# Column sums in place of row sums for two norms, and keys scaled ahead of queries, in a one-core stack of mixers

## The reference, cut to what matters

```python
# gla: 4 heads, keys of 128, values of 256 channels, chunks of 64 tokens
q_dec = q * dk**-0.5 * exp(bcum);  k_inv = k * exp(-bcum);  k_dec = k * exp(b_last - bcum)
o = tril(q_dec @ k_inv.T) @ v + q_dec @ state;  state = state * exp(b_last) + k_dec.T @ v
o = rms_norm(o, o_gain)                      # over the 256 channels of a head, per token
y = (o * silu(z)) @ w_out
# gdn: 4 heads of queries and keys of 128 channels, 8 of values
q = l2_norm(q) * d**-0.5;  k = l2_norm(k)    # over the 128 channels of a head, per token
```

## Time and profile before

| | us |
|---|---|
| median of 3 runs (2366.01 to 2367.77) | 2366.65 |
| the profiled execution's own time | 2366.76 |
| its span, from the first instruction to the last | 2365.0 |
| TensorE busy, of the span | 2293.6 (97%) |
| VectorE, ScalarE, GpSimd busy | 1264.3, 1005.0, 773.2 |

### The profile page before, as it was taken

The page is one execution under the profiler, slowest core; times in us unless marked ns, Lnnn a source line. Parts: engine busy times, 40 slices in busy tenths (PEclk is TensorE's granted clock), DMA queues, the critical chain, the costliest instruction groups (busy, mean ns, idle before and its releaser), DMA issues. The chain is left out here.

```text
span 2365.0 us, 37170 instructions
## 1 busy us (share of the span) xinstructions
PE 2293.6 (97%) x14784; PEld 1947.7 (82%) x14784; DVE 1264.3 (53%) x2094; ACT 1005.0 (42%) x1674; POOL 773.2 (33%) x571
## 2 busy tenths in 40 slices
PE   9999999999999999999999989999999999999998
PEld 7877777878868878877787657999988888999986
DVE  6434246345635545533224774777754344777754
ACT  4335435143444544345424553544524323544522
POOL 3423344133420025333333413111264454111264
PEclk9999999999999999999999999999999999999999
DMA  5333222132210014432222112233233323233232
GB/s 152 72 71 72 82 89 89 37 74 83 89 54 3 3 38 96 92 72 50 87 89 72 64 45 72 90 108 106 89 107 108 104 93 107 90 107 106 89 107 89
DMA packets 137036, 191.93 MB, mean 81 GB/s; under 512 B 31024, under 2 KB 84656, under 8 KB 136896
## 3 DMA queue, kind: packets, MB, share of 16 engines
q1 hardware_dynamic: 128928, 183.64, 26.2%
q10 hardware_dynamic: 7968, 6.32, 0.9%
HBM read 187.84 MB, written 2.10 MB: 80 GB/s over the span
## 5 line engine op out<-in xcount | busy, mean ns | idle before, releaser
L818 POOL TENSOR_TENSOR weights_low<-weights_raw,weights_high 128x512 fp32r<-128x512 f32 x520 | 703.7, 1384 | 1212.7 <-ACT weights_high L1975 1212.6
L1975 ACT ACTIVATE weights_high<-weights_raw 128x1024 fp32r<-128x1024 f32 x260 | 260.9, 1050 | 385.3 <-PE bank L897 379.5
L895 PE MATMUL bank<-xt_high,weights_high 128*128 128x256 f32 (+1 forms) x1152 | 390.1, 339 | 3.9 <-ACT third_sum L2297 1.6
L897 PE MATMUL bank<-xt_high,weights_low 128*128 128x256 f32 (+1 forms) x1152 | 381.9, 332 | 0.0
L896 PE MATMUL bank<-xt_low,weights_high 128*128 128x256 f32 (+1 forms) x1152 | 381.2, 331 | 0.0
L895 PEld LDWEIGHTS bank<-xt_high,weights_high 128*128 128x128 f32 x1152 | 219.3, 190 | 32.9 <-issue 5.6
L897 PEld LDWEIGHTS bank<-xt_high,weights_low 128*128 128x128 f32 x1152 | 219.1, 190 | 21.2
L896 PEld LDWEIGHTS bank<-xt_low,weights_high 128*128 128x128 f32 x1152 | 219.5, 190 | 16.5
L895 PE MATMUL bank<-weights_high,xt_high 128*128 128x512 f32 x432 | 173.9, 403 | 4.9 <-DVE xt_low L2851 2.8
L897 PE MATMUL bank<-weights_high,xt_low 128*128 128x512 f32 x432 | 168.9, 391 | 0.0
L896 PE MATMUL bank<-weights_low,xt_high 128*128 128x512 f32 x432 | 168.7, 391 | 0.0
(11 more groups left out here) (481 smaller groups left out, 4807.0 us busy)
## 6 DMA issues: line engine op xcount, KB each, us to landing
weights_raw<-in_fox_w_in_dram SPq DMA_DIRECT2D x64, 512.0 KB, 5.7
weights_raw<-in_ffn_w_gate_dram SPq DMA_DIRECT2D x44, 512.0 KB, 4.0
weights_raw<-in_ffn_w_up_dram SPq DMA_DIRECT2D x44, 512.0 KB, 4.9
weights_raw<-in_ffn_w_down_dram SPq DMA_DIRECT2D x40, 512.0 KB, 4.3
weights_raw<-in_gla_w_in_dram SPq DMA_DIRECT2D x24, 512.0 KB, 4.5
weights_raw<-in_gdn_w_in_dram SPq DMA_DIRECT2D x24, 512.0 KB, 4.5
weights_raw<-in_attn_w_qkv_dram SPq DMA_DIRECT2D x24, 512.0 KB, 4.5
weights_raw<-in_conv_w_in_dram SPq DMA_DIRECT2D x24, 512.0 KB, 4.2
```

The costliest lines, as they stand in the source:

```text
L818: pool.tensor_tensor(w_lo[:, odd, k], raw[:, odd, k], w_hi[:, odd, k].bitcast(F32), ALU.subtract)\
L895: pe.matmul(out_ap, lh, rh, start=first, stop=False, skip_group_check=skip)
L897: return pe.matmul(out_ap, ll, rh, start=False, stop=last, skip_group_check=skip)
L1975: act.activation(w_hi[:, odd, 2 * m:2 * m + 2], raw[:, odd, 2 * m:2 * m + 2], ACT.Copy)\
```

## The change

- **Sums.** Each squared tile becomes the stationary operand, 128 tokens at a time, and a single column of ones moves (`column_sums`). There are 8 tiles of 4 blocks in each of the two stages, so 32 float32 matmuls with one moving column each. The sums then stand with tokens on the partitions: 128x16 in gla, where both tiles of a head add up in PSUM and DVE's four additions (L3410) go, and 128x32 in gdn.
- **Roots.** ACT does one square root on that tile in place of logarithm and exponential, with its table loaded earlier by `load_root_table`. DVE does a reciprocal, the three Newton operations and the split on 128x16 or 128x32 in place of 4x512 or 8x512 (`norm_columns`).
- **Turned back.** Four transposes on TensorE (`turn_factors`) and a copy of 64x512 from PSUM by DVE (`factor_rows`) bring the factors to rows for the spread, which now has 64 partitions in its contraction.
- **Order in gla.** DVE makes the keys of all heads first and the queries after. TensorE waits for the keys before the transposes and for the queries before `inside(0)`. ACT takes gate 4, loads the root table and squares the first 384 tokens of six tiles before the last output block is there. Gate pieces: (5,1), sums, (6,0), turn, (7,0), spread, (6,1), (7,1). DVE multiplies gates 0 to 2 ahead of the norm, 3 and 4 during it, and 5 after it.
- **Order in gdn.** Sums, values 0 and 1, (4,0), turn, values 2 and 3, spread of four, (4,1), the other values. DVE takes values 0 and 1 inside the norm and 2 and 3 after the first four products. ACT does the root between the two halves of the odd slot's high part.

```diff
+            def column_sums(st, squares, heads, dst):
+                n = max(heads) + 1
+                for k, (tile, h) in enumerate(zip(squares, heads)):
+                    pe.wait_ge(squares_done, st["squares"] + k + 1)
+                    for tt in range(TT):
+                        ins = pe.matmul(dst[:, n * tt + h:n * tt + h + 1], tile[:, tt * P:tt * P + P], ones[:, 0:1],
+                                        start=k == tt == 0, stop=k == len(heads) - 1 and tt == TT - 1,
+                                        skip_group_check=True)
                     ins.then_inc(squares_used, 1)
+            def turn_factors(st, dst):
+                pe.wait_ge(rows_r, st["norms"] + 1)
+                for tt in range(TT):
+                    ins = pe.transpose(dst[0:CHUNK, tt * P:tt * P + P], factor_columns[st["kind"]][:, tt].bitcast(F32), ident[:])
+                ins.then_inc(factors_turned, 1)
...
+                    pe.wait_ge(gla["keys"], 2 * GLA_HEADS)
                     inside(0)
...
                     gate_piece(5, 1)
-                    for h in range(GLA_HEADS):
-                        pe.wait_ge(squares_used, st["squares"] + 2 * h + 2)
-                        ins = pe.matmul(bank[2][0:GLA_HEADS], pick[:, 15 - h:15 - h + GLA_HEADS], buf_c[:, 2 * h],
-                                        start=h == 0, stop=h == GLA_HEADS - 1)
-                    ins.then_inc(gla["norm_sums"], 1)
+                    column_sums(st, [buf_c[:, n] for n in range(8)], [n // 2 for n in range(8)], bank[2])
                     gate_piece(6, 0)
+                    turn_factors(st, bank[2])
                     gate_piece(7, 0)
-                    gate_piece(6, 1)
-                    pe.wait_ge(gla["state"], 8)
-                    pe.wait_ge(rows_r, st["norms"] + 1)
+                    pe.wait_ge(gla["state"], 9)
                     for h in range(GLA_HEADS):
                         spread(st, h, gla["spread"], bank[4 + h])
+                    gate_piece(6, 1)
                     gate_piece(7, 1)
...
-                    norm_sums(st, list(range(8)), 8, bank[1])
+                    column_sums(st, [scratch(st)["squares"][:, n % 2] for n in range(8)], list(range(8)), bank[1])
...
                     gate_piece(4, 0)
+                    turn_factors(st, bank[1])
                     for n in range(2, 4):
                         turn_values(n)
-                    gate_piece(4, 1)
-                    pe.wait_ge(rows_r, st["norms"] + 1)
+                    pe.wait_ge(gdn["selector"], 2)
                     for j in range(4):
                         spread_norms(j)
+                    gate_piece(4, 1)
...
+            def norm_columns(st, sums, n, count, eps, meanwhile):
+                dve.wait_ge(squares_used, st["squares"] + 8)
+                u, y, t = [scratch(st)[name][:, 0:TT * n] for name in ("mean_squares", "reciprocals", "newton")]
+                dve.tensor_scalar(u, sums[:, 0:TT * n], 1.0 / count, eps, ALU.mult, ALU.add).then_inc(root_in, 1)
+                pair = factor_columns[st["kind"]]
                 link(dve.memset(pair[:].bitcast(F32), 0.0))
+                meanwhile()
+                dve.wait_ge(root_out, st["roots"] + 1)
+                link(dve.reciprocal(y, y))
                 link(newton(u, y, t))
+                link(dve.tensor_copy(pair[:, :, 0:n], by_tile(y)))
+                dve.tensor_tensor(pair[:, :, 32:32 + n], by_tile(y), pair[:, :, 0:n].bitcast(F32), ALU.subtract)\
+                    .then_inc(rows_r, 1)
...
                     for h in range(GLA_HEADS):
                         dve.wait_ge(gla["decays"], 2 * h + 2)
-                        link(dve.scalar_tensor_tensor(buf_b[:, h], buf_a[:, h], float(P) ** -.5, decayed[:, h],
-                                                      ALU.mult, ALU.mult))
                         link(dve.tensor_tensor(buf_b[:, 4 + h], buf_a[:, 4 + h], grown[:, h], ALU.mult))
...
+                    for h in range(GLA_HEADS):
+                        dve.scalar_tensor_tensor(buf_b[:, h], buf_a[:, h], float(P) ** -.5, decayed[:, h],
+                                                 ALU.mult, ALU.mult).then_inc(gla["keys"], 1)
...
-                    weights_high(st["pair"] + 1, 1)
-                    inverse_root(st, 0, 8)
+                    half_high(st["pair"] + 1, 1, 0)
+                    root_of_columns(st, 8)
+                    half_high(st["pair"] + 1, 1, 1)
```

More of the change, by code:

```diff
@@ L443, in six_mixer_stack @@
                        "gdn": sb("gdn_factors_high_and_low", 162, [P, SEQ], F32R)}
+        factor_columns = {"gla": sb("gla_factor_columns", 112, [P, TT, CHUNK], F32R),
+                          "gdn": sb("gdn_factor_columns", 160, [P, TT, CHUNK], F32R)}
         cum_pair = sb("gdn_sums_high_and_low", 182, [P, SEQ], F32R)
@@ L508, in six_mixer_stack @@
         rows_r = sem("norm_rows_done")
+        factors_turned = sem("norm_factors_turned")
         first_quadrants = sem("gdn_first_quadrants_done")
@@ L1151, in two_pieces @@
                         ins.then_inc(bank_full, 1)
[L1153 to L1159, removed]
-                    ins.then_inc(squares_used, 1)
+            def column_sums(st, squares, heads, dst):
[6 more added lines that the diff above has]
+                                        skip_group_check=True)
+                    ins.then_inc(squares_used, 1)
+            def turn_factors(st, dst):
[3 more added lines that the diff above has]
+                ins.then_inc(factors_turned, 1)
             def spread(st, n, counter, dst):
-                pe.matmul(dst[:], pair_selector[:, n], factor_pair[st["kind"]][:], start=True, stop=True).then_inc(counter, 1)
+                pe.matmul(dst[:], pair_selector[0:CHUNK, n], factor_pair[st["kind"]][0:CHUNK], start=True, stop=True)\
+                    .then_inc(counter, 1)
             def turn_out(h, gated):
@@ L1988, in root, with load_root_table, root_of_columns @@
                 act.activation(ap, ap, ACT.Sqrt).then_inc(root_out, 1)
[L1990 to L1995, removed]
+            def load_root_table():
+                link(act.activation(stat[:, 31:32], ones[:, 0:1], ACT.Sqrt))
+            def root_of_columns(st, n):
+                u, y = [scratch(st)[name][:, 0:TT * n] for name in ("mean_squares", "reciprocals")]
+                act.wait_ge(root_in, st["roots"] + 1)
+                act.activation(y, u, ACT.Sqrt).then_inc(root_out, 1)
             def square_tiles(st, tiles, base=0, norm=0):
@@ L2514, in _ @@
                             weights_high(st["pair"] + 1, 1)
+                        if tt == TT - 1:
+                            take_gate(4)
+                            load_root_table()
+                            act.wait_ge(gla["out_taken"], 2 * tt)
+                            act.wait_ge(gla["update"], 2 * (2 * tt - 1) + 2)
+                            for n in range(6):
+                                act.activation(buf_c[:, n, 0:tt * P], buf_a[:, n, 0:tt * P], ACT.Square)
                         for g in range(2):
@@ L2523, in _ @@
                     act.wait_ge(gla["out_taken"], 2 * TT)
-                    for n in range(2):
+                    late = slice((TT - 1) * P, SEQ)
+                    act.activation(buf_c[:, 0:6, late], buf_a[:, 0:6, late], ACT.Square).then_inc(squares_done, 6)
+                    for n in range(6, 8):
                         square(n)
-                    take_gate(4)
-                    for n in range(2, 8):
-                        square(n)
+                    root_of_columns(st, GLA_HEADS)
                     take_gate(5)
-                    inverse_root(st, 0, GLA_HEADS)
                     weights_high(st["pair"] + 2, 0)
-                    take_gate(6)
                     for n in range(3):
                         high(st, n)
+                    take_gate(6)
                     weights_high(st["pair"] + 2, 1)
@@ L3407, in _ @@
                     make_selector().then_inc(gla["state"], 1)
-                    for h in range(GLA_HEADS):
-                        dve.wait_ge(squares_done, st["squares"] + 2 * h + 2)
-                        dve.tensor_tensor(buf_c[:, 2 * h], buf_c[:, 2 * h], buf_c[:, 2 * h + 1], ALU.add)\
-                            .then_inc(squares_used, 2)
-                    dve.wait_ge(gla["norm_sums"], 1)
                     def scale_by_gate(*tiles):
@@ L3457, in first_values @@
                     def first_values():
-                        for n in range(4):
+                        for n in range(2):
                             take_values(n)
```

29 lines of the change are left out of this document (16 added, 13 removed).

## The result

The changed kernel takes 2370.64 us (median of 15 runs, 2367.70 to 2373.91), the kernel before 2366.69 us on the same chip (15 runs, 2365.09 to 2368.31). The ratio is 1.0015, with an interval of 1.0008 to 1.0022: slower by 3.95 us, where 2363.2 and a gain were forecast. The time lies inside the stated range (2360.2 to 2371.8), but on the side of rival C. The profiled execution took 2372.41 us, with a span of 2370.3.

The account below looks back on a forecast made before the run. TensorE, busy for 97% of the span, was taken to bound the kernel through its work, waits and clock. gla -4.7 and gdn +1.3 gave -3.4, so 2363.2 us; the 8-in-10 range was 2360.2 to 2371.8.

Parts of the forecast that it names:

- rival C: Both stages: the sums themselves bring the clock down, about 5 us in each; sum +4.6, 2371.3 us; chance 0.30.
- the term of the column sums: Sums in both stages: 64 records at 0.114 us, 7.3 us each; adds 2.85 in gla, 0.25 in gdn.
- Without the long gap the clock stays up: Out projection of gla: first 12 matmuls at full clock take 2.8 us, not 5.2; 2.4 us off.
- A: The forecast itself: gla -4.7, gdn +1.3, sum -3.4 us; own range 2361 to 2365; chance 0.38.
- B: Delta stage: no collision of DVE with POOL, so 0.7 off there; sum -5.4, 2361.2 us; chance 0.24.
- Halving the columns changes nothing: Earlier trace: 64 and 32 moving columns take 0.114 and 0.115 us a record, so the weight load sets the pace.
- the stretch with transposes and a spread: Evidence against C: from 684.6 to 694.0 TensorE stood still 2.8 us of 9.4 and the clock kept 1.00.
- the fall at 861 without a full stop: Evidence for C: from 856 to 865 the clock fell though TensorE stood still only 1.4 us of 9.
- Keys: gla: keys ahead of queries start the key transposes and `inside(0)` 2.3 us earlier, with 0.3 us of room.
- The end of gla: Projection starts at 495.3, 2.3 us earlier, and full clock wins 2.4 more: 4.7 together, the keys' 2.3 included.
- The delta stage: POOL's split slows DVE's small operations, the turn is 1.9 us late: 1.3 on, between 0.7 off and 3 on.

Follow-up runs that it names:

- wide32: The changed kernel with each matmul of the column sums moving 32 columns of ones in place of one: 2369.49 us, ratio 1.0011 to the kernel before.
- wide64: The changed kernel with each matmul of the sums moving 64 columns of ones in place of one, the first kept: 2363.07 us, ratio 0.9985 to the kernel before.
- after_again: The changed kernel, unchanged, measured a second time: 2370.22 us, ratio 1.0016 to the kernel before.
- the kernel with the late split: wide64 with ACT making the odd slot's high part only once DVE has the delta stage's factors: 2361.48 us, repeated 2363.57 us.
- gla_new_gdn_old: The changed kernel with the delta stage's sums, factors, root and order as in the kernel before: 2366.98 us, ratio 1.0001.
- gdn_only: The kernel before with the delta stage's part of the change alone: 2368.64 us, ratio 1.0007.
- wide64_gdn_old: wide64's gla with the delta stage of the kernel before: 2363.43 us, ratio 0.9986 to the kernel before.

## Why the prediction was wrong

- **The step that failed** is the term of the column sums, "64 x 0.114 = 7.3 us in each stage". It carries the pace of full clock through both sums and puts the loss of clock in them, and in the work behind them, at nothing. The runs showed 9.1 and 11.6 us (10.2 and 9.4 in the repeat): 0.112 a record up to the fall, 0.213 behind it, and 0.50 in the gate piece that follows. With 64 columns in place of one the same loads took 7.0 and 7.3 us. "Without the long gap the clock stays up" was right where it was said, at the projection (1.00 from 500.24). The prediction did have the mechanism, as C, at 0.30 against 0.62 for A and B; C's description (first records at 0.11, the rest at 0.21, 0.50 in the gate piece behind) came out as written.
- **Why C was held too low.** The pace came from the earlier trace rows, 16 records in 1.8 us. They show what a load costs, and they are too short to show what the clock does in 7 us of them. "Halving the columns changes nothing" is true for the pace and false for the clock: wide32 fell and wide64 didn't, at the same loads. The evidence against C was the stretch with transposes and a spread at 1.00 in the earlier trace rows; but these move 128 and 512 columns, so they were no likeness of one column. Nor does that stretch always keep the clock: it is where after_again and wide32 fell a third time (693.24, 692.71). The one row that pointed to C was the fall at 861 without a full stop. It pointed the right way, though it too comes and goes: five of the fourteen profiles have it, one of the two of the kernel with the late split among them. The page that the prediction weighed, "TensorE: Matmul & The Clock Gate" of the Trainium skill (The HAM clock gate and PE-mode transpose), made C likelier and was overruled. It says that the clock is set by how busy the engine has been. By the profile's busy share the traces of after don't agree, and they decide here: 100% busy, and 0.50 for 10.24 and 13.65 us. That the page's other remark, on transposes, holds for them is shown by no run.
- **The size of C.** It forecast +0.3 in gla and +4.3 in the delta stage. The trace has -0.2 and +5.75, the medians of gla_new_gdn_old and gdn_only +0.2 and +1.9; the sum of +4.6 compares with +3.95. That the sum comes so near is in part luck: the profiled execution spent 1.5 more than forecast in the delta stage and got 1.3 back because the fall at 861 wasn't there.
- **Keys: right.** 2.3 forecast, 2.2 measured at `inside(0)`, with a small wait for ACT (0.56) that wasn't foreseen and has already been taken off the 2.2.
- **The end of gla: right once the clock stays up.** In wide64 the projection starts at 494.96 without idle time, 2.6 sooner than before (forecast 495.3, 2.3 sooner), and its first 12 matmuls win 2.4 more: 5.0 against 4.7. The sums take 7.0 us, not 7.3.
- **The delta stage: right.** Forecast 1.3 on, a turn 1.9 late by DVE beside POOL; wide64 has 1.2 on and 1.78. B, without the collision, isn't what happens. In after itself the slow clock hides it, and DVE is done 0.6 us before the turn.
- **The whole of A** was therefore -3.4 against a measured -3.7 for wide64: a right sum for another kernel.

Open: why the clock's stretches at 0.50 differ from one execution to the next, and why wide64_gdn_old lost time in runs that weren't profiled. Nothing between 32 and 64 columns was tried. The fall of 3.41 us in the fill behind gla (548.67 to 552.08 in after) costs nothing, since a wait behind it takes it up: before's matmul at 549.6 comes 2.5 us later in after, the one at 555.7 only about 0.7.

## What to carry to other kernels

A stream of matmuls with very few moving columns can be paced by its stationary loads, and TensorE counts as fully busy in it; read the granted clock too, and if it falls, try moving more columns than are needed, as long as the load still hides them. Here 63 wasted columns turned 3 to 4 us lost into 3.7 won. A rival that has a witness in the trace isn't outweighed by a stretch of another kind of work: look for the stretch whose instructions are most like the new ones in the very thing that the rival is about. And where the clock falls in some executions and not in others, one profile gives neither the size of a loss nor the proof that a stretch is safe.

## What was unexpected of the hardware

- TensorE's clock fell to 1.2 GHz while the engine was never idle: 100% busy in the profile, with the loader at 98% or more, 2.3 to 5.3 us after one-column float32 matmuls began. 32 columns per 128x128 load gave the same (3.6 and 4.8 us), 64 did not in any of six profiles.
- The content of the moving columns had no effect: one column of ones and 63 of zeros kept the clock at 1.00 like 64 of ones.
- Three matmuls of 512 columns (0.7 us) after each 1.84 us of one-column ones were not enough to keep it up.
- A small DVE operation with two SBUF inputs took 0.19 us alone and up to 1.2 us beside POOL's 128x512 subtractions, each of which takes 1.25; a reciprocal with one input took 0.34 in both cases.
